# Narrower Fox products, a reordered conv output, seven squares on TensorE, and query units without meta columns, in a three-part model block on one Trainium2 core

## The reference

```python
def short_conv_mixer(h, w_in, conv_w, w_out):
    b, c, xt = jnp.split(h @ w_in, 3, axis=-1)
    u = conv(c * xt, conv_w)                  # causal, width 3, per channel
    return (b * u) @ w_out                    # "cout"

def diff_attention_mixer(h, w_qkv, ...):      # h has 16 meta rows in front
    q, k, v = jnp.split(h @ w_qkv, 3, axis=-1)          # "ain"
    ...                                       # queries of meta rows feed only rows that are dropped
    o = rms_norm(o, subln_g) * (1.0 - lambda_init)
    return o @ w_o                            # "aout"

h = h + rms_norm(m, ln_mix[i, 1])             # sum of squares over the 1024 outputs of cout / aout

def odd_mixer(h, w_in, b_f, qnorm_g, knorm_g, w_out):   # Fox
    q, k, v, g, fl = jnp.split(h @ w_in, ...)           # "oin": 32 units of 128 outputs, and 16 of fl
    q = rms_norm_2(q, qnorm_g);  k = rms_norm_2(k, knorm_g)
    cumf = jnp.cumsum(log_sigmoid(fl + b_f))
    probs = softmax(q @ k.T * scale + cumf_q - cumf_k, causal)
    return ((probs @ v) * silu(g)) @ w_out
```

## Time and profile before

| | us |
|---|---|
| median of 3 runs | 1369.75 (1369.06 to 1372.03) |
| profiled execution | 1367.15 |
| its span, first to last instruction | 1365.3 |
| TensorE busy with matmuls | 1322.7 (97%) |
| VectorE busy | 919.1 (67%) |
| ScalarE busy | 811.8 (59%) |
| GpSimd busy | 103.9 (8%) |
| mean granted clock of TensorE | 0.984 of 2.4 GHz |

### The profile page before, as it was taken

How to read it: one execution, slowest core, us unless ns; L and a number is a source line. 1 busy time by engine, 2 the same in 40 slices (tenths; PEclk the granted TensorE clock), 3 DMA queues, 4 the chain that set the end, 5 groups by cost and what they waited for, 6 DMA issues and landing times.

```text
span 1365.3 us, 27462 instructions
## 1 busy us (share of the span) xinstructions
PE 1322.7 (97%) x10198; PEld 1279.7 (94%) x10198; DVE 919.1 (67%) x1519; ACT 811.8 (59%) x1575; POOL 103.9 (8%) x119
## 2 busy tenths in 40 slices
PE   7999999999999999999999999799999899989998
PEld 7999999998999999999999898799999899977888
DVE  7877546866877645877645777578864575566765
ACT  7766634446776645776645565677774453556774
POOL 2000001002000002000002211210001100000000
PEclk9999998999999999999999999899999999989999
DMA  7767653654777743777742543367775253345441
GB/s 252 243 222 224 227 183 119 188 154 137 231 230 229 235 152 117 237 230 222 242 153 84 155 130 97 124 199 237 242 259 179 86 169 110 109 149 171 130 124 63
DMA packets 64609, 240.49 MB, mean 176 GB/s; under 512 B 7904, under 2 KB 9360, under 8 KB 64528
## 3 DMA queue, kind: packets, MB, share of 16 engines
q1 hardware_dynamic: 63312, 238.77, 54.8%
q0 software_dynamic: 1216, 0.60, 0.2%
HBM read 237.70 MB, written 1.05 MB: 175 GB/s over the span
## 4 chain that ended last, share of the span: by engine, by line
PE 84%; DVE 7%; ACT 5%; DMA 2%; issue 1%; POOL 1%; SPq 0%; ACTq 0%; DVEq 0%; POOLq 0%
PE bank L1851 22%; PE bank L1853 22%; PE bank L1852 22%; PE bank L1858 4%; DVE w_lo L1120 2%; PE bank L1859 2%; ACT w_hi L612 1%; PE bank L1923 1%; ACT ada_raw L698 1%; PE bank L1924 1%; PE bank L1916 1%; PE bank L2221 1%; DMA raw<-w 1%; DVE h L1182 1%; ACT x_hl L653 1%
## 5 line engine op out<-in xcount | busy, mean ns | idle before, releaser
L1120 DVE TENSOR_TENSOR w_lo<-raw,w_hi 128x1024 fp32r<-128x1024 f32 (+2 forms) x376 | 488.7, 1304 | 236.6 <-ACT w_hi L612 236.5
L1851 PE MATMUL bank<-x_hl,w_hi 128*128 128x272 f32 (+1 forms) x1776 | 515.0, 290 | 4.8 <-DVE x_hl L1188 4.1
L1853 PE MATMUL bank<-x_hl,w_lo 128*128 128x272 f32 (+1 forms) x1776 | 511.4, 288 | 0.0
L1852 PE MATMUL bank<-x_hl,w_hi 128*128 128x272 f32 (+1 forms) x1776 | 509.6, 287 | 0.0
L612 ACT ACTIVATE w_hi<-raw 128x1024 fp32r<-128x1024 f32 (+2 forms) x376 | 409.8, 1096 | 147.4 <-PE bank L1853 130.9
L1851 PEld LDWEIGHTS bank<-x_hl,w_hi 128*128 128x128 f32 x1776 | 335.9, 189 | 6.3 <-ACT x_hl L653 4.1
L1852 PEld LDWEIGHTS bank<-x_hl,w_hi 128*128 128x128 f32 x1776 | 338.6, 191 | 0.4
L1853 PEld LDWEIGHTS bank<-x_hl,w_lo 128*128 128x128 f32 x1776 | 335.4, 189 | 0.0
L1851 PE MATMUL bank<-a_hi,w_hi 128*128 128x272 f32 (+1 forms) x960 | 278.5, 290 | 4.2 <-DVE a_lo L1367 1.8
L1853 PE MATMUL bank<-a_hi,w_lo 128*128 128x272 f32 (+1 forms) x960 | 274.7, 286 | 0.0
L1852 PE MATMUL bank<-a_lo,w_hi 128*128 128x272 f32 (+1 forms) x960 | 274.1, 286 | 0.0
(11 more groups left out here) (280 smaller groups left out, 1415.4 us busy)
## 6 DMA issues: line engine op xcount, KB each, us to landing
raw<-w SPq DMA_DIRECT2D x312, 512.0 KB, 4.3
raw<-w SPq DMA_DIRECT2D x64, 704.0 KB, 4.5
ada_raw<-ada_w SPq DMA_DIRECT2D x48, 512.0 KB, 3.5
h<-x_in SPq DMA_DIRECT2D x2, 544.0 KB, 5.4
work<-bands SPq DMA_DIRECT2D x1, 544.0 KB, 6.3
arena<-arena POOLq DMA_DIRECT2D x32, 17.0 KB, 3.5
out<-h SPq DMA_DIRECT2D x1, 512.0 KB, 2.9
out<-h SPq DMA_DIRECT2D x4, 128.0 KB, 2.3
```

What stands on the lines that cost most here:

```text
L1120: ve.tensor_tensor(w_lo[:, s, cols], raw[:, s, cols], w_hi[:, s, cols].bitcast(F32), ALU.subtract).then_inc(w_lo_ready, 1)
L1851: te.matmul(dst, w_hi[:, s, a:a + P], rhs_hi, start=first, stop=False)
L1852: te.matmul(dst, w_hi[:, s, a:a + P], rhs_lo, start=False, stop=False)
L1853: return te.matmul(dst, w_lo[:, s, a:a + P], rhs_hi, start=False, stop=last)
```

## The change

- **Fox projection**: `product_halves`, `project_halves`, `whole` and `fox_first` go. Each chunk is a `product` of three 256-column matmuls, ScalarE copies the finished unit out of the bank's first 256 columns (`fox_evict`), and what waited for VectorE's addition waits for that copy. The stage begins with `first_quad`. Units 9 and 10 use banks 7 and 3, and `fox_freed` says which unit's copy has to be done before a bank is written again. From unit 14 on `fox_evict` also waits for the reader of the buffer that it overwrites, two pairs earlier.
- **Conv output**: seven chunks of unit 0, seven of unit 1, then the eighth of unit 0 and of unit 1, then units 2 and 3 and the second quad as before.
- **Attention output**: GpSimd adds six squares; TensorE waits for the sixth addition, and adds the square of the seventh unit with a ones-matmul of its own.
- **Query units** from unit 6 on are made with columns 16 to 271 only.

```diff
         def fox_bank(u):
-            return bank[{2: 7, 3: 3}.get(u, u % 2)]
+            return bank[{2: 7, 3: 3, 9: 7, 10: 3}.get(u, u % 2)]
+        def fox_freed(u):
+            return {4: 0, 5: 1, 9: 2, 10: 3, 11: 7, 12: 8}.get(u, u - 2)
...
+        def pool_adds(n):
+            return 6 if n == "aout" else 7
...
             def raw_q(h):
                 att_done(3 * h)
-                sc.activation(q_raw[h % 2], (bank[3] if h == 1 else bank[3 * h % 2])[:, 0:T], ACT.Copy
-                              ).then_inc(act.step(f"q{h}", "q"), 1)
+                src = bank[3][:, META:T] if h == 1 else bank[3 * h % 2][:, 0:SEQ]
+                sc.activation(q_raw[h % 2][:, META:T], src, ACT.Copy).then_inc(act.step(f"q{h}", "q"), 1)
...
-            def lower_half(u):
+            def fox_evict(u):
                 sc.wait_ge(unit_done, SLOTS * FIRST_QUAD["oin"] + u + 1)
-                sc.activation(fox_unit(u), fox_bank(u)[:, SEQ:2 * SEQ], ACT.Copy).then_inc(act.step(f"c{u}", "c"), 1)
+                if u >= GATES + 6:
+                    j, kind = divmod(u - GATES, 3)
+                    if kind == 2:
+                        sc.wait_ge(pe.sem, pe.at(f"fn{j - 2}", "vt"))
+                    else:
+                        sc.wait_ge(vec.sem, vec.at(f"fqk{j - 2}", "qk"[kind]))
+                sc.activation(fox_unit(u), fox_bank(u)[:, 0:SEQ], ACT.Copy).then_inc(act.step(f"c{u}", "c"), 1)
             def fox_square(name, j, u, e):
-                sc.wait_ge(vec.sem, vec.at(f"d{u}", "d"))
+                sc.wait_ge(act.sem, act.at(f"c{u}", "c"))
...
-            def whole(u):
-                ve.wait_ge(act.sem, act.at(f"c{u}", "c"))
-                ve.tensor_tensor(fox_unit(u), fox_unit(u), fox_bank(u)[:, 0:SEQ], ALU.add).then_inc(vec.step(f"d{u}", "d"), 1)
...
-                for o in range(7):
+                for o in range(pool_adds(stage)):
...
-            out1("cout", "resc", k_ready=lambda k: (vec.sem, vec.at("cin0" if k == 0 else f"cin{3 * k + 2}", f"lo{k}")))
+            def cout_part(s, chunks):
+                te.wait_ge(w_lo_ready, SLOTS * FIRST_QUAD["cout"] + s + 1)
+                for k in chunks:
+                    te.wait_ge(vec.sem, vec.at("cin0" if k == 0 else f"cin{3 * k + 2}", f"lo{k}"))
+                    last = product(bank[s][:, 0:T], s, k, a_hi[:, k, 0:T], a_lo[:, k, 0:T], k == 0, k == DC - 1)
+                if k == DC - 1:
+                    last.then_inc(unit_done, 1)
+            def cout_last():
+                for s in range(SLOTS):
+                    te.wait_ge(w_lo_ready, SLOTS * FIRST_QUAD["cout"] + SLOTS + s + 1)
+                    te.wait_ge(act.sem, act.at("cout", f"f{s}", 0))
+                    for k in range(DC):
+                        if s == 3 and k == 5:
+                            res_most("resc", pool.at("cout", "add6"))
+                        last = product(bank[s][:, 0:T], s, k, a_hi[:, k, 0:T], a_lo[:, k, 0:T], k == 0, k == DC - 1)
+                    last.then_inc(unit_done, 1)
+                res_last("resc", act.at("cout", "sq3", 1))
+            cout_part(0, range(0, 7))
+            cout_part(1, range(0, 7))
+            cout_part(0, range(7, 8))
+            cout_part(1, range(7, 8))
+            cout_part(2, range(0, 8))
+            cout_part(3, range(0, 8))
+            cout_last()
...
-                unit("ain", bank[u % 2], u % SLOTS, T)
+                t0 = 0 if u % 3 else META
+                for k in range(DC):
+                    last = product(bank[u % 2][:, 0:T - t0], u % SLOTS, k, x_hi[:, k, t0:T], x_lo[:, k, t0:T], k == 0, k == DC - 1)
+                last.then_inc(unit_done, 1)
...
                         if s == 3 and k == 5:
                             te.wait_ge(act.sem, act.at("aout", "f0", 1))
-                            res_most("resa", pool.at("aout", "add6"))
+                            res_most("resa", pool.at("aout", "add5"))
+                            te.wait_ge(act.sem, act.at("aout", "sq2", 1))
+                            te.matmul(STAT[:, 0:SEQ], ones[:, :], sq[:, 0, 0:SEQ], start=False, stop=False)
...
                 if u >= 4:
-                    te.wait_ge(vec.sem, vec.at(f"d{u - 2 if u > 5 else u - 4}", "d"))
-                for k in range(DC):
-                    last = product_halves(fox_bank(u)[:, :], u % SLOTS, k, x_hl[:, k, :, 0:SEQ], k == 0, k == DC - 1)
-                last.then_inc(unit_done, 1)
+                    te.wait_ge(act.sem, act.at(f"c{fox_freed(u)}", "c"))
+                unit("oin", fox_bank(u), u % SLOTS, SEQ)
...
-            fox_first()
-            fox_project(3)
+            first_quad("preo", "oin", SEQ, (bank[0], bank[1], bank[7]))
```

More of the change, by code:

```diff
@@ L311, in declare_ffn @@
             pe.phase(d, ["ada"])
+        def pool_adds(n):
+            return 6 if n == "aout" else 7
         def declare_out1(n, res):
             act.phase(n, ["sq0", "f0", "sq1", "f1", "sq2", "f2", "sq3", "f3"], 2)
-            pool.phase(n, ["zero"] + [f"add{o}" for o in range(7)])
+            pool.phase(n, ["zero"] + [f"add{o}" for o in range(pool_adds(n))])
             declare_res(res)
@@ L443, in build @@
             act.phase(f"c{u}", ["c"])
-            vec.phase(f"d{u}", ["d"])
             if u == 3:
@@ L476, in build @@
             u = GATES + 3 * p
-            if pair(p):
-                vec.phase(f"d{u}", ["d"])
             if pair(p - 2):
@@ L486, in build @@
                 vec.phase(f"fqk{p - 1}", ["q", "k"])
-            if pair(p):
-                vec.phase(f"d{u + 1}", ["d"])
-                vec.phase(f"d{u + 2}", ["d"])
             if pair(p - 1):
@@ L1070, in _ @@
             for u in range(GATES):
-                lower_half(u)
+                fox_evict(u)
                 fox_split_hi(u)
@@ L1663, in _ @@
             for u in range(GATES):
-                whole(u)
                 fox_split_lo(u)
@@ L1752, in _ @@
                 if pair(p):
-                    whole(u + 1)
                     fox_split_lo(u + 1)
-                    whole(u + 2)
                     fox_split_lo(u + 2)
@@ L1853, in product @@
                 return te.matmul(dst, w_lo[:, s, a:a + P], rhs_hi, start=False, stop=last)
-            def product_halves(dst, s, w, both, first, last):
-                a = w * P
-                te.matmul(dst.rearrange("p (a t) -> p a t", a=2), w_hi[:, s, a:a + P], both, start=first, stop=False)
-                return te.matmul(dst[:, 0:SEQ], w_lo[:, s, a:a + P], both[:, 0, :], start=False, stop=last)
-            def project_halves(stage, free, k_ready):
-                def quad(i):
-                    q = FIRST_QUAD[stage] + i
-                    for s in range(SLOTS):
-                        te.wait_ge(w_lo_ready, SLOTS * q + s + 1)
-                        if not isinstance(i, int) or i > 0:
-                            te.wait_ge(*free(s, i - 1))
-                        for k in range(DC):
-                            if isinstance(i, int) and i == 0 and s == 0:
-                                te.wait_ge(*k_ready(k))
-                            last = product_halves(bank[s][:, :], s, k, x_hl[:, k, :, 0:SEQ], k == 0, k == DC - 1)
-                        last.then_inc(unit_done, 1)
-                quads(stage, quad)
             def quads(stage, body):
@@ L2019, in evac_free @@
                 return lambda s, i: (act.sem, act.at(stage, f"e{s}", i))
-            def out1(stage, res_, ready=None, k_ready=None):
-                project(stage, width(stage), a_hi, a_lo, lambda s, i: (act.sem, act.at(stage, f"f{s}", i)),
-                        t0=toks(stage).start, after=ready, k_ready=k_ready,
-                        halfway=lambda: res_most(res_, pool.at(stage, "add6")))
-                res_last(res_, act.at(stage, "sq3", 1))
             te.wait_ge(pool.sem, pool.at("setup", "ones"))
@@ L2337, in fox_project @@
                 if u >= 4:
-                    te.wait_ge(vec.sem, vec.at(f"d{u - 2 if u > 5 else u - 4}", "d"))
-                for k in range(DC):
-                    last = product_halves(fox_bank(u)[:, :], u % SLOTS, k, x_hl[:, k, :, 0:SEQ], k == 0, k == DC - 1)
-                last.then_inc(unit_done, 1)
-            def fox_first():
-                te.wait_ge(w_lo_ready, SLOTS * FIRST_QUAD["oin"] + 3)
-                for k in range(DC):
-                    te.wait_ge(vec.sem, vec.at("preo", f"lo{k}"))
-                    for u in range(3):
-                        last = product_halves(fox_bank(u)[:, :], u, k, x_hl[:, k, :, 0:SEQ], k == 0, k == DC - 1)
-                        if k == DC - 1:
-                            last.then_inc(unit_done, 1)
+                    te.wait_ge(act.sem, act.at(f"c{fox_freed(u)}", "c"))
+                unit("oin", fox_bank(u), u % SLOTS, SEQ)
             def fox_sums(j):
```

8 lines of the change are left out of this document (4 added, 4 removed).

## The result

| | before | changed |
|---|---|---|
| median (lowest to highest), runs beside each other | 1369.72 us (1366.85 to 1372.03), 6 runs | 1358.49 us (1358.39 to 1359.05), 6 runs |
| profiled execution: time, span | 1367.15, 1365.3 us | 1358.39, 1356.6 us |
| mean granted clock in it | 0.984 | 0.986 |

The ratio is 0.9923, with a 95% interval from 0.9908 to 0.9938: 11.2 us less in this comparison, and 8.8 us between the two profiled executions. The forecast was 1361 us. So the size of the gain depends on which runs one meets: 8 to 11 us, and the two comparisons' intervals overlap.

The account below looks back on a forecast made before the run. TensorE, busy 97% of the span, was taken as the bound. Gains 2.0 + 1.5 + 1.0 + 3.4 + 1.6 = 9.5 us less 1.0 us loss: 1369.75 - 8.5 = 1361.25, rounded 1361 us; range 1357.0 to 1366.0 us.

Parts of the forecast that it names:

- Position: Conv output: other chunks' matmuls fill TensorE's pause before unit 0's eighth chunk; 2.0 us gained.
- clock: Conv output: the low-clock stretch right behind the pause goes with it; 1.5 us gained, bounds nothing and 1.7 us.
- Forms: Matmul shapes: narrow Fox products lose 1.0 us, six attention query units with 256 columns instead of 272 gain 1.0 us.
- rival (6): Fox products: the third weight load isn't hidden, 0.192 us each, 49 us at most, up to 1410 us; chance 0.01.
- Fox head: Start of the Fox stage: two pauses, a late start and slow first products go; 3.4 us gained.
- The first pause: Fox head: unit 7's wait for VectorE's addition of unit 5 goes; 1.17 us gained.
- The tight place: Fox head: ScalarE has the second square at 1247.5, unit 10's copy at 1247.8, before sums at 1248.0; else up to 1.5 us lost.
- Rival (2): Fox head: a new wait behind ScalarE's table loads and Silu, up to 1.5 us lost, 1362.5 us; chance 0.12.
- (4): Attention: softmax waits take the query units' 1.0 us, something else ends the output pause; 1363.5 to 1367.5 us; chance 0.11.
- (5): Fox periods: ScalarE becomes the bound; at 1.7 us a period 1374.6 us, slower; chance 0.03.
- The offset: Whole kernel: before's timed median lies 2.6 us above its profiled execution, kept for the changed kernel.
- Rival (3): Fox pauses too bring low-clock stretches in timed runs, so 2 to 3 us more are given back, 1358.5 us; chance 0.08.

Follow-up runs that it names:

- run 10: The changed kernel with spare products, read by nobody, wherever TensorE stands for over 2 us; 1356.42 us.
- runs 2 and 3: The changed kernel with the conv output's old order, 1363.42 us; the same with 14 spare products ahead of the wait for chunk 7, 1362.92 us.
- run 8: The changed kernel with the Fox stage's first three units started chunk by chunk, as before, instead of upper parts first; 1360.82 us.
- run 5: The changed kernel with Fox units 9 and 10 in the banks of before (1 and 0); 1362.82 us.
- run 1: The changed kernel again, unaltered, nine runs beside before; 1361.85 us against 1369.62 us.
- run 4: The changed kernel with the whole Fox projection of before, the rest of the change kept; 1363.25 us.

## Why the prediction was right

**The bound.** That only TensorE's stream and its pauses count held: each of the five places where TensorE's stream changed shows its share in the offsets, and the other engines' work was hidden, but for the 1.1 us of run 10, where split weights came too late for a faster TensorE.

**Conv output.** Position 2.1 us (said: 2.0), clock 1.55 (said: 1.5). Both parts are shown, by runs 2 and 3. The granted clock behind it is 1.00, as the last part of the prediction asked.

**Forms.** Query units: 0.20 us a unit, 1.2 in all (said: 0.17 and 1.0). Narrow Fox products: pair to pair the period grew by 0.125 us, where three units at 0.004 us a product make 0.096; by that 0.005 us a product, 1.3 us in all (said: 1.0). The third weight load is hidden, so rival (6) is out. The Trainium skill ("TensorE: Matmul & The Clock Gate", Back-to-back issue gap) would have had 16 us more, by an estimate from its figures for streams with weight loads; in the trace after, 256 columns stay 118 ns apart, so it doesn't bear them out.

**Fox head.** Said 3.4 us gross. From the stage's start to pair 0's sums the traces show 2.9 net, and with twelve units at 0.005 us a product 3.4 gross. Of that the start is 0.3 (run 8), the pause that the banks remove 1.2 of 1.75 (run 5). The first pause (1.17 us) wasn't taken back alone; it is argued from the earlier trace rows and from the wait that is gone. The tight place held, with the margins that were forecast: ScalarE's second square ended at 1240.95, 0.5 us ahead of the sums at 1241.45 (said: 0.5), and the copy of unit 10 at 1241.22, 0.2 us ahead (said: 0.2). ScalarE's rows after, table loads, Silu and the copies of units 9 and 10:

```profile
1234.48 1.28 ACT L1091 ACT_TABLE_LOAD   x1
1235.77 1.92 ACT L1093 ACTIVATE arena<-arena 128x2048 f32<-128x2048 f32 x1
1237.71 1.28 ACT L1094 ACT_TABLE_LOAD   x1
...
1239.32 0.37 ACT L1038 ACTIVATE arena<-bank 128x256 f32<-128x256 f32 x1
...
1240.54 0.41 ACT L1042 ACTIVATE sq<-arena 128x256 f32<-128x256 f32 x1
1240.84 0.38 ACT L1038 ACTIVATE arena<-bank 128x256 f32<-128x256 f32 x1
```

Rival (2) is out, and so are (4), of which every term stands in the table, and (5): between pair 0's scores and 1324 us TensorE stands nowhere (74.50 of 74.50 us).

**Attention output.** Said 1.6, measured 1.6 up to the sum. 0.5 us more came up to the next products, where I had counted the clock as unchanged: before had a low stretch of 10.2 us there, the changed kernel 3.4. Whether these 0.5 us are the edit's or chance is not shown: run 1 had 6.8 us there for the same changed kernel and lost nothing by it against the first trace.

**The sum against the profile.** 1367.15 - 8.5 = 1358.7 us was forecast for a profiled execution, 1358.39 measured. That it fits so well is in part luck: both traces have GpSimd's short sums (6.4 us). The changed kernel's second profiled execution took 1360.76 us, by which the gain is 6.4.

**The offset.** The 2.6 us that I kept between profile and median is the one term whose size no row gave. In the first six runs of the changed kernel it is 0.1 us, and that is 2.5 of the 2.8 us between 1361.25 and 1358.49; the other 0.3 is the sum's. In the nine runs of experiment 1 it would be 3.5 over the first profile and 1.1 over their own, and 1361.85 is 0.6 from the forecast, and that nearness is in part chance. The explanation that I gave it in brackets (low-clock stretches fall differently) is borne out for before; for the changed kernel it is half of it, beside GpSimd's sums. Rival (3), that the change takes the offset away, had the first six runs' time to the tenth (1358.5 us), and yet its mechanism isn't borne out: the kernel spreads again, from 1358.8 to 1363.9 us, and the old Fox pauses brought no low stretch (run 4). What decides whether a pause gets 3.4 or 6.8 us at the low level in one execution stays open, and so does why the first six runs lie within 0.7 us.

## What to carry to other kernels

Cost an edit on a full engine by its position first, and then look at the granted clock right behind the pause that it removes: here a pause of 1.8 us cost 2.1 us of position and 1.55 more of clock. Keep a saving that one profiled execution shows apart from the spread between executions, and repeat the kernel itself before reading a median that lies 2 or 3 us off. Where TensorE has to stand for 2 us or more, products that nobody reads were worth 2 to 5 us here, up to 0.4%, depending on which runs they are compared with. And before a loss of 1 or 2 us in one trace is laid to an edit, look at the same place in two traces of the unaltered kernel.

## What the runs showed that I had not expected

The same kernel, at the same places, gets low-clock stretches of 3.4 or of 6.8 us (875.9 to 879.3 us in one execution, 875.1 to 881.9 in another), and this makes most of the 9 us between before's fastest and slowest run. Fourteen spare products, 1.92 us long, in a pause of 1.82 us of idle time kept the clock at its upper level for what followed, at no cost in time (2.11 us lost with them, 3.65 without). GpSimd's addition of 128 x 256 took 0.73 us at 862.13 and 1.52 us at 866.26, in the same kernel. Its three additions of 128 x 1088 ahead of the swap DMA took 6.44 us in one execution of that kernel and 7.44 in another, and TensorE's longest wait of the attention moved from 3.4 to 5.2 us with them.
